# Weights of a hybrid decoder layer laid out in memory tile by tile, one 512 KB load for each

## The reference

```python
h = rms_norm(x, norm_w)
proj = jnp.einsum('btd,de->bte', h, w_in)          # w_in: 2048 x 8204
# 4 retention heads, 6 gated-DeltaNet heads, 6 block-sparse attention heads, width 128 each
...
y = jnp.concatenate([y_ret, y_gdn, y_moba], axis=-1)
return x + jnp.einsum('bte,ed->btd', y, w_out)     # w_out: 2048 x 2048
```

## Time and profile before

| | before |
|---|---|
| median of 3 runs | 511.75 us (511.47 to 512.03) |
| the profiled execution, its own time | 511.29 us |
| its span, first to last instruction | 509.5 us |
| matrix engine busy | 504.4 us, 99% |
| VectorE, ScalarE, GpSimd busy | 342.9, 275.5, 162.3 us |
| moved by DMA | 92.62 MB, mean 182 GB/s |

### The profile page before, as it was taken

The page is one execution under the profiler, slowest core; times in us unless marked ns, Lnnn a source line. Parts: engine busy times, 40 slices in busy tenths (PEclk is TensorE's granted clock), DMA queues, the critical chain, the costliest instruction groups (busy, mean ns, idle before and its releaser), DMA issues.

```text
span 509.5 us, 8939 instructions
## 1 busy us (share of the span) xinstructions
PE 504.4 (99%) x3442; PEld 424.6 (83%) x3442; DVE 342.9 (67%) x529; ACT 275.5 (54%) x452; POOL 162.3 (32%) x220
## 2 busy tenths in 40 slices
PE   8999999999999999999999999999999999999997
PEld 7888888888888888888888888888888888888885
DVE  5989999989776876565467455755567566646451
ACT  5776565754357676564537354564556456343340
POOL 5763343416121312135054105506050614230000
PEclk9999999999999999999999999999999999999999
DMA  8997656665744465563975676777775557767711
GB/s 283 344 313 207 166 133 165 185 173 142 200 124 130 126 165 144 146 183 69 303 185 156 160 221 169 187 207 195 186 193 169 166 172 231 219 186 225 256 43 41
DMA packets 154989, 92.62 MB, mean 182 GB/s; under 512 B 15971, under 2 KB 143938, under 8 KB 154946
## 3 DMA queue, kind: packets, MB, share of 16 engines
q1 hardware_dynamic: 151456, 89.86, 63.3%
q10 hardware_dynamic: 3490, 2.18, 1.5%
HBM read 89.00 MB, written 2.10 MB: 179 GB/s over the span
## 4 chain that ended last, share of the span: by engine, by line
PE 99%; POOL 0%; DVE 0%; DVEq 0%; issue 0%; POOLq 0%
PE pj L1554 20%; PE pj L1557 20%; PE pj L1556 20%; PE pj L1532 14%; PE pj L1533 7%; PE pj L1610 3%; PE pj L1619 1%; PE mx L1714 1%; PE pj L1529 1%; PE mx L1581 1%; PE mx L1749 1%; PE mx L1767 1%; PE pj L1627 1%; PE mx L1825 1%; PE mx L1887 1%; PE pj L1528 1%
## 5 line engine op out<-in xcount | busy, mean ns | idle before, releaser
L369 DVE TENSOR_TENSOR w_lo<-w_raw,w_hi 128x1024 fp32r<-128x1024 f32 x160 | 200.0, 1258 | 78.0 <-ACT w_hi L489 77.3
L489 ACT ACTIVATE w_hi<-w_raw 128x1024 fp32r<-128x1024 f32 x158 | 166.1, 1057 | 120.5 <-PE pj L1557 103.7
L1554 PE MATMUL pj<-w_hi,hT 128*128 128x512 f32 x320 | 126.4, 395 | 0.0
L1556 PE MATMUL pj<-w_hi,hT 128*128 128x512 f32 x320 | 126.1, 394 | 0.0
L1557 PE MATMUL pj<-w_lo,hT 128*128 128x512 f32 x320 | 124.7, 390 | 0.0
L1532 PE MATMUL pj<-hT,w_hi 128*128 128x512 f32 x300 | 109.3, 404 | 0.0
L1533 PE MATMUL pj<-hT,w_lo 128*128 128x256 f32 x300 | 83.9, 280 | 0.0
L1557 PEld LDWEIGHTS pj<-w_lo,hT 128*128 128x128 f32 x320 | 60.1, 188 | 12.2
L1554 PEld LDWEIGHTS pj<-w_hi,hT 128*128 128x128 f32 x320 | 60.1, 188 | 12.1
L1556 PEld LDWEIGHTS pj<-w_hi,hT 128*128 128x128 f32 x320 | 60.2, 188 | 11.5
L1532 PEld LDWEIGHTS pj<-hT,w_hi 128*128 128x128 f32 x300 | 56.3, 188 | 14.1 <-DVE w_lo L369 1.6
(11 more groups left out here) (238 smaller groups left out, 537.6 us busy)
## 6 DMA issues: line engine op xcount, KB each, us to landing
w_raw<-in_w_in_dram SPq DMA_DIRECT2D x256, 256.0 KB, 3.3
w_raw<-in_w_out_dram SPq DMA_DIRECT2D x64, 256.0 KB, 4.0
big<-in_x_dram SPq DMA_DIRECT2D x9, 256.0 KB, 5.6
out_dram<-sq ACTq DMA_DIRECT2D x7, 256.0 KB, 5.8
big<-in_x_dram SPq DMA_DIRECT2D x3, 512.0 KB, 7.1
cst<-table_dram SPq DMA_DIRECT2D x1, 682.0 KB, 9.7
kq<-vr SPq DMA_DIRECT2D x32, 16.0 KB, 1.8
kq<-mT SPq DMA_DIRECT2D x24, 16.0 KB, 1.9
```

What stands on the lines that cost most here:

```text
L369: eng.tensor_tensor(w_lo[:, n % NSPLIT, :], w_raw[:, n % NRAW, :], w_hi[:, n % NSPLIT, :].bitcast(F32), ALU.subtract).then_inc(S("lo"), 1)
L489: act.activation(w_hi[:, n % NSPLIT, :], w_raw[:, n % NRAW, :], ACT.Copy).then_inc(S("hi_done"), 1)
L1554: ins = pe.matmul(bank[:, :], src[:, kc, 0, tok], hi[:, k, :], start=first, stop=False)
L1556: pe.matmul(bank[:, :], src[:, kc, 1, tok], hi[:, k, :], start=False, stop=False)
```

## The change

The host lays the weights out as an array `tiles` of 160 x 128 x 1024 float32, in the order of their use, and passes it in the place of `w_out`; in the place of `w_in` it passes the 12 gate columns alone. A tile is then 512 KB without a gap, and a partition's row of it is one piece of 4 KB. Tiles 0 and 1 are still loaded as two halves, now with pieces of 2 KB; every other tile is one transfer, and ScalarE waits for 16 instead of 32 counts of its semaphore. The numbers, their places in the buffers, and the arithmetic on all engines are the same. The gate columns are still loaded by ScalarE's queue as 2048 pieces of 48 bytes, now out of an array that holds nothing else.

```diff
--- before.py
+++ after.py
+def weight_tiles(w_in, w_out):
+
+    tiles = np.empty((TILES, P, TK * 512), np.float32)
+    for n in range(TILES):
+        group, q = tile_at(n)
+        rows = slice(q * TK * P, (q + 1) * TK * P)
+        if group >= HEADS:
+            g = group - HEADS
+            tile = w_out[0, rows, g * 512:(g + 1) * 512].reshape(TK, P, 512)
+        elif group == 0:
+            tile = w_in[0, rows, GDN_COL:GDN_COL + 2 * GDN * P].reshape(TK, P, 2, GDN * P)[:, :, :, 0:2 * P]
+        elif group < GDN:
+            p, h, i = section(group, q // 2)
+            at = GDN_COL + (i * GDN + 2 * p + h) * P
+            tile = w_in[0, q % 2 * UPT * P:(q % 2 + 1) * UPT * P, at:at + P].reshape(UPT, P, P)
+        else:
+            kind, j = PAIRS[group // 2]
+            heads, col = {"ret": (RET, RET_COL), "moba": (MOBA, MOBA_COL)}[kind]
+            h = 2 * j + group % 2
+            tile = w_in[0, rows, col:col + 4 * heads * P].reshape(TK, P, 4, heads * P)[:, :, :, h * P:(h + 1) * P]
+        tiles[n] = np.moveaxis(tile, 0, 1).reshape(P, TK * 512)
+    return tiles
...
             def load(n):
-                group, q = tile_at(n)
-                rows = slice(q * TK * P, (q + 1) * TK * P)
+                if n < 2:
+                    for k, done in enumerate((f"w_first{n}", f"w_in{n}")):
+                        cols = slice(k * 512, (k + 1) * 512)
+                        sp.dma_start(w_raw[:, n, cols], tiles[n, :, cols]).then_inc(S(done), 16)
+                    return
                 if n >= NRAW:
                     wait_lo(sp, n - NRAW)
-                dst = w_raw[:, n % NRAW, :].rearrange("p (k n) -> p k n", k=TK)
-                if group < HEADS:
-                    kind, j = PAIRS[group // 2]
-                    heads = {"gdn": GDN, "ret": RET, "moba": MOBA}[kind]
-                    first_col = {"gdn": GDN_COL, "ret": RET_COL, "moba": MOBA_COL}[kind]
-                    h = 2 * j + group % 2
-                    if group == 0:
-                        done = [S(f"w_first{n}"), S(f"w_in{n}")] if n < 2 else [S(f"w_in{n % NRAW}")] * TK
-                        src = w_in[0, rows, GDN_COL:GDN_COL + 2 * GDN * P].rearrange("(k p) (i c) -> p k i c", p=P, i=2)[:, :, :, 0:2 * P]
-                        dst = dst.rearrange("p k (i c) -> p k i c", i=2)
-                        for k in range(TK):
-                            sp.dma_start(dst[:, k], src[:, k]).then_inc(done[k], 16)
-                    elif group >= GDN:
-                        src = w_in[0, rows, first_col:first_col + 4 * heads * P].rearrange(
-                            "(k p) (s c) -> p k s c", p=P, s=4)[:, :, :, h * P:(h + 1) * P]
-                        dst = dst.rearrange("p k (s c) -> p k s c", s=4)
-                        for k in range(TK):
-                            sp.dma_start(dst[:, k], src[:, k]).then_inc(S(f"w_in{n % NRAW}"), 16)
-                    else:
-                        p, h, i = section(group, q // 2)
-                        at = GDN_COL + (i * GDN + 2 * p + h) * P
-                        rows = slice(q % 2 * UPT * P, (q % 2 + 1) * UPT * P)
-                        src = w_in[0, rows, at:at + P].rearrange("(k p) c -> p k c", p=P)
-                        dst = w_raw[:, n % NRAW, :].rearrange("p (k c) -> p k c", k=UPT)
-                        for k in range(0, UPT, UPT // TK):
-                            sp.dma_start(dst[:, k:k + UPT // TK], src[:, k:k + UPT // TK]).then_inc(S(f"w_in{n % NRAW}"), 16)
-                else:
-                    g = group - HEADS
-                    src = w_out[0, rows, g * 512:(g + 1) * 512].rearrange("(k p) c -> p k c", p=P)
-                    for k in range(TK):
-                        sp.dma_start(dst[:, k], src[:, k]).then_inc(S(f"w_in{n % NRAW}"), 16)
+                sp.dma_start(w_raw[:, n % NRAW, :], tiles[n]).then_inc(S(f"w_in{n % NRAW}"), 16)
...
             def high_part(n):
-                act.wait_ge(S(f"w_in{n % NRAW}"), 16 * TK * (n // NRAW + 1) - (16 if n % NRAW < 2 else 0))
+                act.wait_ge(S(f"w_in{n % NRAW}"), 16 * (n // NRAW + 1))
...
-                    act.dma_start(wab[:, :, 0:AB], w_in[0, :, AB_COL:AB_COL + AB].rearrange("(k p) c -> p k c", p=P)).then_inc(S("wab_in"), 16)
+                    act.dma_start(wab[:, :, 0:AB], gate_w.rearrange("(k p) c -> p k c", p=P)).then_inc(S("wab_in"), 16)
...
+    laid_out = {name: _np.asarray(inputs[name]) for name in _INS}
+    laid_out["w_out"] = weight_tiles(laid_out["w_in"], laid_out["w_out"])
+    laid_out["w_in"] = laid_out["w_in"][0, :, AB_COL:AB_COL + AB]
     for name in _INS:
-        a = _np.ascontiguousarray(inputs[name])
+        a = _np.ascontiguousarray(laid_out[name])
```

More of the change, by code:

```diff
@@ L133, in constants, with tile_at, section, layer @@
     return t.astype(np.float32)
-def layer(nc, x, norm_w, w_in, conv_w, a_log, dt_bias, ret_norm_w, gdn_norm_w, q_norm_w, k_norm_w, w_out,
+def tile_at(n):
+    if n < HEADS * TPH:
+        return n // TPH, n % TPH
+    g, q = OUT_TILES[n - HEADS * TPH]
+    return HEADS + g, q
+def section(g, s):
+    return g % 3, s % 2, 2 * (g // 3) + s // 2
+def weight_tiles(w_in, w_out):
[19 more added lines that the diff above has]
+    return tiles
+def layer(nc, x, norm_w, gate_w, conv_w, a_log, dt_bias, ret_norm_w, gdn_norm_w, q_norm_w, k_norm_w, tiles,
           table, out):
@@ L268, in col @@
             return sm[:, a:b] if i is None else sm[:, a + i:a + i + 1]
-        def section(g, s):
-            return g % 3, s % 2, 2 * (g // 3) + s // 2
         def raw_of(p, h, i, cols=slice(0, PAD + T)):
@@ L290, in layer @@
         qT = kq[:, 1].rearrange("p c k t -> p (c k t)")
[L292 to L297, removed]
         def in_rows(p):
```

## The result

The changed kernel is slower: 514.39 us in the median of 12 runs (512.77 to 519.62), the kernel before 511.58 beside it. The ratio is 1.0062, with a 95% interval of 1.0049 to 1.0075. In a later series the same changed kernel had 513.40 in 5 runs, beside 511.62, a ratio of 1.0031 (1.0019 to 1.0044). So the loss is 1.6 to 3.2 us by the ratios, and it varies more than the time of the kernel before does. Five of the 12 runs of the first series (515.43 to 519.62 us) had a granted clock of 0.993 to 0.997, the other seven and the whole second series 0.999 or 1.00; the median of the seven is 513.92. The profiled execution took 513.92 us.

The account below looks back on a forecast made before the run. The prediction took the matrix engine's own work to bound the kernel, with weight loads early. Start, steady part and side effects, each 0, left the profiled execution at 511.3 us and the median at 511.7, range 510.9 to 512.5.

Parts of the forecast that it names:

- The bound: Whole kernel: the matrix engine, busy 504.4 of 509.5 us, is paced by its own work; loads come early.
- the steady part: Steady weight loads: a tile is eaten in 2.72 us, loads needing only 193 GB/s; effect 0.
- Larger pieces: Weight loads: 1.61 us a tile, at most 1.88, under the 2.72 us needed; DMA share falls, end unchanged.
- Fewer issues on SP: SP's queue: 320 weight loads become 162, SP has 244.9 us to spare, order of work unchanged; value 0.
- the matrix engine itself waits only for VectorE's `w_lo`: Reading of the waits before the change: 1.6 us in 6 cases, used to show loads are early.
- the rule on row distances: Skill's rule: copies with rows a large power of two apart ran at 207 to 103 GB/s; counted under rival "Slower".
- The start: First half tile's load, the only place where a load ends a wait: 0, bounds -0.08 to +0.8 us.
- Slower: Rival: new array read at a lower rate, deciding from 193 GB/s down; 539 us at 180 GB/s; chance 0.04.
- The sum: Whole kernel: start 0, steady part 0, side effects 0 (-1.6 to +0.8 us); median 511.7 us.
- the case for no change: Likeliest case, 511.7 us: only one wait in the whole trace ends with a weight load; chance 0.90.

Follow-up runs that it names:

- the one of 0.9995: Changed kernel with gate columns in 128 pieces of 2 KB and halves of tiles 0 and 1 in 2 KB pieces, rows 32 KB apart: 511.70 us.
- the other places: Changed kernel, 128 gate pieces, halves of tiles 0 and 1 in rows 32 KB apart: 511.83 us from the old wide matrix, 511.70 from an own array.
- the start alone mended: Changed kernel with halves of tiles 0 and 1 in 2 KB pieces, rows 32 KB apart, gate load unchanged on ScalarE's queue: 512.97 us, 1.0034.

## Why the prediction was wrong

**The bound, and the steady part: right.** The matrix engine's pace was 2.72 us a tile before and 2.74 after, no weight load was waited for behind 32 us, the waits for `w_lo` stayed as they were (1.4 us against 1.6), the packets fell to 38,028 (forecast about 40,000), the share of the weight queue to 51.5% (forecast 55% or lower). The runs with 4 KB pieces behind tile 10 alone, or early alone, and the one of 0.9995 show that the steady part adds nothing that can be told.

**The step that failed** is the term "Larger pieces", where I wrote that "The DMA share should fall, the end should not". I priced a 4 KB piece for the weight queue alone and put what it costs the pieces of another queue at nothing, without a reason. The reason given under "Fewer issues on SP", that no transfer is moved past a longer queue and the bytes ahead of each are equal, looks at one queue too. (The number of issues did cost nothing, as I had it: with one load for a tile and small or 2 KB pieces the stop is gone.) ScalarE's queue has loads of its own, and the rows of ScalarE that I showed began and ended with the first weight tile. What the runs showed in its place: the 2048 gate pieces landed after 21.7 us instead of 12.3, ScalarE, with 0.4 us to spare before, stood at its next issue for 5.67 us instead of 2.71, and the matrix engine lost 1.5 us near 21 us.

The trace before had the warning: ScalarE's issue row of 2.71 us, and the gate load with 12.3 us to landing for 96 KB. Also, "the matrix engine itself waits only for VectorE's `w_lo`" was not a full reading: the same view has one wait for GpSimd of 1.3 us and one for a load, `norm_w` on ScalarE's queue, of 0.7.

I should have priced it. 2048 pieces over 16 engines are 128 for each, and if each waits for one weight piece, then a piece of 4 KB costs what this row of the changed kernel's weight queue says (packets, MB and share in the window 6 to 32 us, to be laid beside the earlier trace rows):

```profile
q1 hardware_dynamic: 3464, 9.41, 93.6%
```

9.41 MB in 93.6% of 26 us are 387 GB/s, 24 for one of the 16 DMA engines; 4 KB are 0.17 us there, and 128 times that 21.7 us. That this is the measured landing to the digit is luck. The landing has 3.6 us in it before the first small piece moves, and the passage itself took 17.5, since only 0.8 large pieces pass for each small one and a part of them are pieces of 2 KB of x. But the size is right, and the same two parts make up the landing before: 3.5 us until the first small piece moves and 8.5 us of passage, 12.3 in all.

The Trainium skill has the rule, on the same page that I cited for another: "DMA: Bandwidth & Descriptors", section "Queues, rings and completion order", says that each DMA engine goes round the queues it has work for and changes only at packet boundaries. The landing of 20.1 to 21.8 us in four profiles with 4 KB pieces throughout, against 12.3 to 13.8 with small ones, agrees with it as far as these loads go, and so do the counts of about one large piece for each small one; how many pieces make a turn no run shows. The rule speaks against this change, and I weighed only the rule on row distances.

**The start: mechanism named, size and cause off.** I gave the first half tile 0, with bounds of -0.08 and +0.8 us. It landed at 5.65 us in the profile of the changed kernel instead of 5.31, and at 4.78 to 6.40 in the others of its layout; the first product moved by 0 to 1.1 us. The reason, that pieces of 2 KB are no smaller than those of 1 KB, was beside the point: the rate in the first microseconds went with where they lie. The rival "Slower", a lower read rate, was right in kind, but only for these four half loads; over the whole run the weight queue was faster, not slower (89.85 MB in 51.5% of 512.1 us, 341 GB/s, against 279). What 2 KB in every 4 KB meets in memory no run shows. How much the start cost in the medians stays open: with 128 gate pieces the other places brought the ratio from 1.0018 to 1.0000 and 0.9995, but with the gate load moved to SP's queue the start of the changed kernel had no loss left to mend (0.9999), and the start alone mended brought nothing clear.

**The sum.** By the profiles the stop costs 1.5 to 1.8 us and the start 0 to 1.1, together 1.5 to 2.9; the medians lie 1.8 and 2.8 us over the kernel before. The chance of 0.04 for slower was far too small: the case for no change rested on the single wait that ends with a weight load, which was read rightly and did not cover the loads of others.

**Left open.** Why five of the 12 runs of the first series had the lower granted clock. None of them left a trace, the other seven and the second series had none of it, and the run with the gate load last had it once in 11 (514.78 us, 0.997). Also open is what ends ScalarE's stand: it ended 4.9 us after the gate load's issue before and 8.0 in the changed kernel, and then 390 and 570 of the 2048 pieces had started, so it is not a fixed number of them.

## What to carry to other kernels

When a transfer's pieces get larger, look at every other queue in that stretch, above all for a load of many short pieces and for what its engine does right behind the issue: here few large pieces, or the queue that carries the big ones, ended ScalarE's stand, while issuing the load last on the engine that computes only moved the wait to whoever needs the data. A wait that shows as "issue" can be a transfer in disguise, as ScalarE's 3.44 us here: look for the ACTq or SPq row over it, and at how much cover it has, before saying that transfers are hidden. And a load layout has two numbers, the size of a piece and the distance to the next; change one at a time at the start of a kernel, where the first load is bare.

## What the runs showed of the hardware

- 2048 pieces of 48 bytes on ScalarE's queue took 12.3 to 13.8 us to land beside weight pieces of 512 bytes to 1 KB, 17.0 beside 2 KB, and 20.1 to 21.8 beside 4 KB; 128 pieces with 2.7 times the bytes took 5.9. The next issue on the same queue stood for 2.7 to 3.6, 3.9 and 5.0 to 6.0 us (the 5.0 with 4 KB up to tile 10 alone). While the 2048 passed, 0.8 to 1.3 times as many pieces of the other queue did.
- While the first tiles were loaded as pieces of 2 KB at a distance of 4 KB, all transfers together brought 193 to 209 GB/s in the window 4 to 6 us; at a distance of 32 KB 284 to 332.
- One 512 KB block read in pieces of 1 KB, 128 KB apart for one partition, gave 330 and 334 GB/s in the window 6 to 15 us, and the same pieces spread over a wide matrix 365 and 370.
